# A hybrid recurrent trunk on one core: norm roots in two pieces among z's slabs, FFN tiles split in one pipeline, the result turned by halves

## The reference

```
def _gdn_mixer(x, conv0, S0, P, j):
    proj = x @ P['gdn_w_in'][j]                  # q | k | v | z | beta, decay
    qkv, conv_new = _causal_conv(proj[..., :GDN_CONV_DIM], conv0, P['gdn_conv_w'][j])
    qkv = silu(qkv)
    q = _l2norm(q heads) * GDN_DK ** -0.5
    k = _l2norm(k heads)
    ...
    o, S = _gated_delta_chunked(q, k, v, g, beta, S0)
    o = _rmsnorm(o, P['gdn_norm_w'][j]) * silu(gate)      # gate is z
    return o @ P['gdn_w_o'][j], conv_new, S

def _conv_ffn(x, conv0, P, i):
    h, conv_new = _causal_conv(x @ P['ffn_w_up'][i], conv0, P['ffn_conv_w'][i])
    return (silu(h[..., D_FF:]) * h[..., :D_FF]) @ P['ffn_w_down'][i], conv_new
```

## Time and profile before

| | |
|---|---|
| timed runs | 2292.86, 2284.80, 2296.56 us; median 2292.86 |
| the profiled execution | 2283.04 us; span from first to last instruction 2281.3 us |
| mean granted clock of TensorE | 0.939 |
| busy share of the span | PE 90%, PEld 83%, DVE 65%, ACT 43%, POOL 24% |
| DMA | 257.77 MB, mean 113 GB/s |
| GDN's input projection | ends near 788 us |
| the four FFNs start | near 387, 954, 1432 and 2040 us |
| the last residual tile | near 2270.6 us |

### The profile page before, as it was taken

One profiled execution on the slowest core, in us unless ns is written; L12 is line 12 of the kernel. 1 busy time (PEld: TensorE's weight loads), 2 busy tenths in 40 slices (PEclk: granted clock), 3 DMA queues, 4 the chain that ended last, 5 costly groups with the idle time before them and its releaser, 6 DMA issues.

```text
span 2281.3 us, 54685 instructions
## 1 busy us (share of the span) xinstructions
PE 2055.3 (90%) x23459; PEld 1891.9 (83%) x23459; DVE 1483.9 (65%) x2211; ACT 974.1 (43%) x1657; POOL 550.4 (24%) x934
## 2 busy tenths in 40 slices
PE   4999988999899787899989797999979899789997
PEld 3898867999778675799979776899958788679997
DVE  4785454896467556499645674898267655549963
ACT  3641134554456303455535434555345411345543
POOL 8000000453023211046201450365000200005520
PEclk9999998999989879899999888999979899989999
DMA  3430122555333323255535253354434101225542
GB/s 97 145 117 23 30 67 76 165 164 163 115 100 123 114 61 90 76 165 166 164 121 159 92 164 120 111 167 158 131 94 152 65 22 32 69 74 167 167 154 79
DMA packets 272112, 257.77 MB, mean 113 GB/s; under 512 B 30708, under 2 KB 267222, under 8 KB 271870
## 3 DMA queue, kind: packets, MB, share of 16 engines
q1 hardware_dynamic: 221472, 219.49, 30.0%
q10 hardware_dynamic: 45870, 20.44, 3.4%
q0 software_dynamic: 4528, 14.33, 2.3%
HBM read 235.69 MB, written 18.54 MB: 111 GB/s over the span
## 4 chain that ended last, share of the span: by engine, by line
PE 53%; DVE 6%; ACT 3%; issue 2%; ACTq 1%; POOL 0%; DMA 0%; DVEq 0%; POOLq 0%
PE wide L537 7%; PE wide L538 7%; PE wide L539 7%; PE bank L537 7%; PE bank L539 6%; PE bank L538 6%; DVE arena L2519 3%; PE wide L548 1%; PE wide L737 1%; DVE arena L2516 1%; PE wide L722 1%; PE wide L734 1%; ACT arena L1744 1%; PE bank L488 1%; PE wide L488 1%
## 5 line engine op out<-in xcount | busy, mean ns | idle before, releaser
L2519 DVE TENSOR_TENSOR w_lo<-ring,w_hi 128x2048 fp32r<-128x2048 f32 (+1 forms) x208 | 477.9, 2299 | 301.0 <-ACT w_hi L1744 298.1
L537 PE MATMUL wide<-arena_rounded,w_hi 128*128 128x288 f32 x1632 | 497.5, 305 | 51.6 <-DVE arena_rounded L2519 35.1
L537 PE MATMUL bank<-arena_rounded,w_hi 128*128 128x288 f32 x1632 | 491.2, 301 | 11.4 <-issue 11.4
L538 PE MATMUL wide<-arena_rounded,w_hi 128*128 128x288 f32 x1632 | 490.4, 300 | 0.0
L539 PE MATMUL wide<-arena_rounded,w_lo 128*128 128x288 f32 x1632 | 488.8, 300 | 0.0
L538 PE MATMUL bank<-arena_rounded,w_hi 128*128 128x288 f32 x1632 | 486.3, 298 | 0.0
L539 PE MATMUL bank<-arena_rounded,w_lo 128*128 128x288 f32 x1632 | 485.1, 297 | 0.0
L1744 ACT ACTIVATE w_hi<-ring 128x2048 fp32r<-128x2048 f32 (+1 forms) x208 | 391.6, 1884 | 141.1 <-PE bank L539 71.4
L537 PEld LDWEIGHTS wide<-arena_rounded,w_hi 128*128 128x128 f32 x1632 | 315.1, 193 | 64.9 <-issue 41.6
L537 PEld LDWEIGHTS bank<-arena_rounded,w_hi 128*128 128x128 f32 x1632 | 311.1, 191 | 12.8 <-issue 11.9
L2516 DVE SCALAR_TENSOR_TENSOR arena<-arena,pv 128x304 f32<-128x304 f32 (+2 forms) x512 | 303.3, 602 | 25.1 <-ACT arena L1744 9.6
(11 more groups left out here) (486 smaller groups left out, 2698.8 us busy)
## 6 DMA issues: line engine op xcount, KB each, us to landing
ring<-in_ffn_w_up SPq DMA_DIRECT2D x88, 1024.0 KB, 5.1
ring<-in_ffn_w_down SPq DMA_DIRECT2D x32, 896.0 KB, 4.7
ring<-in_rwkv_w_rkv SPq DMA_DIRECT2D x24, 1024.0 KB, 5.3
ring<-in_ffn_w_down SPq DMA_DIRECT2D x16, 1024.0 KB, 5.1
ring<-in_gdn_w_in SPq DMA_DIRECT2D x16, 1024.0 KB, 5.7
ring<-in_hgrn_w_in SPq DMA_DIRECT2D x16, 1024.0 KB, 5.4
ring<-in_rwkv_w_o SPq DMA_DIRECT2D x8, 1024.0 KB, 5.1
sraw<-in_state_rwkv_wkv POOLq DMA_DIRECT2D x32, 128.0 KB, 3.1
```

Source lines behind the costliest of these rows:

```text
L537: nc.tensor.matmul(out, wh, xh, start=first, stop=False)
L538: nc.tensor.matmul(out, wh, xl, start=False, stop=False)
L2519: return V.tensor_tensor(out, a, b, op)
```

## The change

Three edits. In GDN, ScalarE's roots move from behind tile 21 to behind the last silu of v, and are made in two pieces, `SQ` and `H` apart: both Ln behind the table load, then the evacuations of tiles 26 and 27 and slab 15's high half, then both Exp, and only then the staging of the conv state. z is evacuated as it is, and one silu over all of `S[8]` follows its last tile. On VectorE `norm_q_k` is gone; slab 15's low half stands ahead of the operands, and q and k are multiplied by their roots there. In the FFN the multiplications and subtractions of the eight tiles are interleaved, a subtraction two tiles behind. At the end the halves are the outer loop: the first halves of all three blocks need only four residual tiles; six banks are used, the third block is staged in `sout`, and the wait for the first two transfers is gone.

```diff
@@ TensorE, the end
-            pe.wait_ge(sem("x_ready"), after(pe, "x_ready", 2 * DEPTH * KC))
-            for blk, n in enumerate((P, P, NS)):
-                for q in range(2):
-                    b = 2 * (blk % 2) + q
+            for q in range(2):
+                pe.wait_ge(sem("x_ready"), (2 * DEPTH - 1) * KC + 4 * (q + 1))
+                for blk, n in enumerate((P, P, NS)):
+                    b = 3 * q + blk
                     pe.wait_ge(*freed(b))
@@ ScalarE, gdn
                     if n == 21:
                         raw_stats(H)
-                        log_and_exp()
-                        both = flat("H", 2)
-                        fn(both, both, ACT.Ln, bias=eps[:, 0:1]).then_inc(signal("scalar_chain"), 1)
-                        act.wait_ge(sem("scalar_chain"), told["scalar_chain"])
-                        fn(both, both, ACT.Exp, scale=-0.5).then_inc(signal("rk_ready"), 1)
-                        act.wait_ge(sem("rk_ready"), told["rk_ready"])
-                evac(S[8][:, 0, :], ACT.Silu)
                 qkv(GT - 2)
-                evac(S[8][:, 1, :], ACT.Silu)
+                evac(S[8][:, 0, :])
+                evac(S[8][:, 1, :])
                 split_hi(n0 + 14)
                 qkv(GT - 1)
+                log_and_exp()
+                for x in (SQ, H):
+                    fn(x, x, ACT.Ln, bias=eps[:, 0:1]).then_inc(signal("scalar_chain"), 1)
                 act.wait_ge(sem("saved"), after(act, "saved", 4))
-                evac(S[8][:, 2, :], ACT.Silu)
-                evac(S[8][:, 3, :], ACT.Silu)
+                evac(S[8][:, 2, :])
+                evac(S[8][:, 3, :])
                 split_hi(n0 + 15)
+                act.wait_ge(sem("scalar_chain"), told["scalar_chain"])
+                for x in (SQ, H):
+                    fn(x, x, ACT.Exp, scale=-0.5).then_inc(signal("rk_ready"), 1)
                 conv_state_out(OUT["prompt_gdn_conv"][0], OUT["sample_gdn_conv"][0], 72, 3)
                 for c in range(4, KC):
-                    evac(S[8][:, c, :], ACT.Silu)
+                    evac(S[8][:, c, :])
+                fn(S[8], S[8], ACT.Silu).then_inc(signal("z_gate"), 1)
+                act.wait_ge(sem("z_gate"), told["z_gate"])
                 log_and_exp()
@@ ScalarE, the end
-                if blk == 2:
-                    act.wait_ge(sem("y_out"), 32)
...
+            for q in range(2):
+                for blk, n in enumerate((P, P, NS)):
                     act.wait_ge(filled["scalar"], take())
-                    fn(tm[0:n, g, q * 512:(q + 1) * 512], psb()[0:n, :], ACT.Copy).then_inc(drained["scalar"], 1)
+                    fn(stages[blk][0:n, q * 512:(q + 1) * 512], psb()[0:n, :], ACT.Copy).then_inc(drained["scalar"], 1)
                     act.wait_ge(drained["scalar"], n_taken["n"])
...
+                    if q:
+                        act.dma_start(rows_out[blk], stages[blk][0:n, :]).then_inc(sem("y_out"), 16)
@@ VectorE, ffn
-                pre_norm("ffn_pre", i, "h_to_split")
-                for c in range(KC):
-                    dve.wait_ge(sem("x_hi"), after(dve, "x_hi"))
-                    tt(act3r("H")[:, c, :], H[:, c, :], act3r("A4")[:, c, :], ALU.subtract).then_inc(signal("x_split"), 1)
+                dve.wait_ge(sem("rstd_ready"), after(dve, "rstd_ready"))
+                for step in range(KC + 2):
+                    if step < KC:
+                        stt(H[:, step, :], X[:, step, :], pcol("ffn_pre", i, step), rstd[:, :]).then_inc(signal("h_to_split"), 1)
+                    if step >= 2:
+                        dve.wait_ge(sem("x_hi"), after(dve, "x_hi"))
+                        tt(act3r("H")[:, step - 2, :], H[:, step - 2, :], act3r("A4")[:, step - 2, :],
+                           ALU.subtract).then_inc(signal("x_split"), 1)
@@ VectorE, gdn
-                    if n == 22:
-                        norm_q_k()
...
-                tt(QG, Q, EG).then_inc(signal("vector_chain"), 1)
+                split_lo(n0 + 15)
+                dve.wait_ge(sem("rk_ready"), after(dve, "rk_ready"))
+                stt(Q, Q, float(P) ** -0.5, SQ).then_inc(signal("vector_chain"), 1)
+                dve.wait_ge(sem("vector_chain"), told["vector_chain"])
+                tt(QG, Q, EG)
+                dve.wait_ge(sem("rk_ready"), after(dve, "rk_ready"))
+                tt(K, K, H).then_inc(signal("vector_chain"), 1)
                 dve.wait_ge(sem("vector_chain"), told["vector_chain"])
                 stt(EG, K, -1.0, EG).then_inc(signal("operands_ready"), 1)
                 dve.wait_ge(sem("operands_ready"), told["operands_ready"])
-                split_lo(n0 + 15)
@@ VectorE, gated
-                    dve.wait_ge(drained["scalar"], mark["gin", 31] + 1)
+                    dve.wait_ge(sem("z_gate"), 1)
```

More of the change, by code:

```diff
@@ L2477, in _ @@
             ffn(3)
-            y = tm[:, :, :]
             hear_conv_out()
-            for blk, n in enumerate((P, P, NS)):
-                g = blk % 2
-                if blk == 2:
-                    act.wait_ge(sem("y_out"), 32)
-                for q in range(2):
+            hear_state_out()
+            stages = (tm[:, 0, :], tm[:, 1, :], sout)
+            rows_out = (OUT["y_prompt"][0][0:P], OUT["y_prompt"][0][P:2 * P], OUT["y_sample"].rearrange("b t f -> (b t) f"))
+            for q in range(2):
+                for blk, n in enumerate((P, P, NS)):
                     act.wait_ge(filled["scalar"], take())
-                    fn(tm[0:n, g, q * 512:(q + 1) * 512], psb()[0:n, :], ACT.Copy).then_inc(drained["scalar"], 1)
+                    fn(stages[blk][0:n, q * 512:(q + 1) * 512], psb()[0:n, :], ACT.Copy).then_inc(drained["scalar"], 1)
                     act.wait_ge(drained["scalar"], n_taken["n"])
-                dst = OUT["y_prompt"][0, blk * P:blk * P + n] if blk < 2 else OUT["y_sample"].rearrange("b t f -> (b t) f")
-                act.dma_start(dst, tm[0:n, g, :]).then_inc(sem("y_out"), 16)
+                    if q:
+                        act.dma_start(rows_out[blk], stages[blk][0:n, :]).then_inc(sem("y_out"), 16)
             act.wait_ge(sem("y_out"), 48)
@@ L3032, in exponents @@
                 dve.wait_ge(sem("exponents_ready"), told["exponents_ready"])
-            def norm_q_k():
-                dve.wait_ge(sem("rk_ready"), after(dve, "rk_ready"))
-                stt(S[1], S[1], float(P) ** -0.5, SQ)
-                tt(S[4], S[4], H).then_inc(signal("vector_chain"), 1)
-                dve.wait_ge(sem("vector_chain"), told["vector_chain"])
             def masks(hb, q):
```

## The result

The changed kernel takes 2267.11 us in the median of 8 runs, the kernel before 2290.03 in 8 runs of the same comparison: a ratio of 0.9914, 95% interval 0.9890 to 0.9939, or 14 to 25 us less. (The ratios here are those on record for each comparison; they aren't the quotients of the two medians, which lie 22.9 us apart here, and microseconds given with an interval go by the ratio.) 2279 (2270 to 2290) was forecast, so the kernel is faster, as the likeliest class said, but by more than the 11.9 us of the sum, and the time lies 2.9 us under the range.

A forecast was written before the change was run, and what follows sets the result against it. TensorE, busy 90% of the span, was taken as the bound, so time is won only where it stands still or runs slow. Gains of 6.4 + 1.2 + 4.3 = 11.9 us gave 2279 us from 2290.9, range 2270 to 2290.

The forecast's parts named there:

- the likeliest class: Whole kernel: faster by over 0.5%, chance 0.51, against 0.46 for within 0.5% and 0.03 for slower.
- the 11.9 us of the sum: Whole kernel: gains of 6.4 us in GDN, 1.2 in four FFNs and 4.3 at the end; bounds 8.7 to 13.3.
- The clock's 1.9 us: GDN, slabs 14 and 15: time lost to TensorE's 1.2 GHz clock after the long stop, taken between 1.4 and 2.4 us.
- 766.4: GDN: time in us at which slab 14 was to start on TensorE, after ScalarE's staging starts at 765.6.
- the lower bound of nothing: FFN starts: gain of 0 instead of 1.2 us, if the clock rises at a fixed time anyway.
- The bound of 2.8: The end: gain of only 2.8 us if the last transfer starts only when the block before it has landed.
- the one of 4.8: The end: upper bound, a gain of 4.8 us if TensorE's clock stays up through the turn.
- (1): GDN: VectorE becomes the bound, two of four products at 5.89 us; whole gain 7.3 us, 2283.6 us; chance 0.06.
- (2): GDN: GpSimd busy throughout, split and four products take 27.5 us; kernel 1.1 us slower, 2292.0 us; chance 0.03.
- The clock (4): GDN: clock stays at 1.2 GHz through both slabs after the long stop; whole gain 3.1 us, 2287.8; chance 0.02.
- the two rows 4: Profile rows cited for TensorE's clock after stops: 0.53 over 3.22 us in GDN, 0.50 over 5.40 us at an FFN's start.
- Rival (3): GDN: table switch holds ScalarE longer, staging 1.3 us later; whole gain 10.6 us, 2280.3 us; chance 0.07.

The follow-up runs named there:

- the version with the roots on both sides: Changed kernel with query roots ahead of the conv state's staging, key roots behind it, query product before slab 15's split: 2265.34 us (0.9925), again 2270.59 us (0.9938).
- the trace with five products: Changed kernel with one VectorE product in GDN (the gated query) made twice in a row: 2273.72 us in 1 run.
- the second and the third comparison: Changed kernel rerun unaltered against the kernel before: 2271.05 us for 2283.34 (0.9934), then 2271.97 us for 2284.04 (0.9947).
- GDN alone: Kernel before with only the change's GDN edit (roots, z, slab 15's split): 2280.30 us for 2283.34, ratio 0.9985.
- the rest alone: Kernel before with the FFN and end edits, without the GDN edit: 2278.06 us for 2284.04, ratio 0.9974.
- the version with the roots behind the staging: Changed kernel with ScalarE's staging of the conv state ahead of both Ln and both Exp: 2272.24 us for 2285.60, ratio 0.9947.

## Why the prediction was right, and where it was not

**GDN, 6.4 forecast, 6.7 measured.** Matmul starts of the two traces are 3.1 us apart at the start of the stage. With that, slab 13's split was put to end at 752.0 and ended at 752.0; ScalarE's staging was put at 765.6 + 3.1 = 768.7 and came at 768.45; the stop was put at about 9 us and is 8.60; the inversion was put at 781.75 + 3.1 = 784.85 and came at 784.60. The clock's 1.9 us is what the window shows, but that it fits is luck: it was picked between 1.4 and 2.4 with no row to decide, and the premise that the clock is low after such stops holds for some of them only. Behind the kernel before's own 2.22 us stop the clock stayed at 1.00, and behind the 2.84 us stop of the version with the roots on both sides 3.05 us were lost. A small slip is hidden as well: 766.4 leaves 0.28 us for the three transposes behind the staging, which take 0.51 (768.97 to 769.48), and the staging came 0.25 us earlier than put. The products ended 1.0 us before slab 15 (783.95), where 1.4 was forecast, and 1.7 before the inversion.

**FFN, 1.2 forecast, 1.2 measured at the first matmul.** Later in the stage it is less steady. From the start of that wait to the 41st matmul of the second FFN the five traces without the edit have 12.69 to 12.73 us; of the nine with it four have 12.51 to 12.55, so 0.2 of the 0.3 stay there, two 12.28 and 12.36, and three 11.33 to 11.45. Nothing of it can be seen at the end of a longer stretch: from the inversion's first matmul to the 15486th, in which the second and the third FFN start, the two traces with the FFN edit and GDN's roots in their old place take 810.6 and 810.7 us, the four without the edit 810.6 to 810.8. So the size is right at the starts, but whether it reaches the end isn't shown, and the lower bound of nothing stands.

**The end, 4.3 forecast, 3.9 measured.** The last issue comes 3.97 us after the last residual tile (2271.03 less 2266.60 + 0.46), where it came 8.35 us after it (2278.94 less 2270.59): 4.4 less, as worked out. The span goes on for 2.85 us after that issue where it went on for 2.37, so 0.5 was lost behind it, put down here to transfers issued close together, which no run tests by itself, and for which 0.1 had been set aside. That term was mis-sized, by 0.4 us. The bound of 2.8 (the last transfer behind the one before it) was not met; the one of 4.8 (the clock up through the turn) nearly was, once: in the trace with five products the twelve transposes behind the last tile take 1.53 us for 2.82, and the end is 4.4 us shorter than before.

**The rivals.** VectorE's products ran at 2.5 to 2.56 us each, so neither (1) nor (2) came about; GpSimd waits for slab 15 for 26.57 us there, as it did before. The clock (4) was back after 3.76 us; the two rows 4, which the prediction set against it, stop where the low stretch does and hardly show its return. Rival (3) fell as well: after the table load at 756.22, 1.28 us, the Ln begins at 757.51, 0.01 us behind its end, and ScalarE was busy up to 756.22. The Trainium skill (ScalarE: Activation LUTs, "What ACT_TABLE_LOAD costs") gives 1283 ns for the load, which agrees, and about 1380 ns of drain for every switch, which isn't in any trace here. The same section prices an ACTIVATE higher when its bias is read from a per-partition operand: the Ln with eps takes 2.21 to 2.22 us and the Exp, which has none, 2.12 to 2.13 in the version with the roots apart.

**What missed is the time, through the scatter that the range left out.** The step was "I predict 2279 us, which lies between the two and puts the kernel before at 2290.9", with a range drawn from "the fastest timed run less the largest gain". The base was right for the comparison that it was made for: the kernel before came out at 2290.03. What the forecast missed there is the difference, 14 to 25 us by the ratio for 11.9, and "some gain above 13.3 that I have not seen" had a chance of only 0.03. The later comparisons speak for chance in the two medians of 8 as most of it. In them the kernel before has medians of 2283 to 2286 and the changed one 2271 to 2272, so in the first comparison the one came out 4 to 7 us high and the other 4 to 5 us low. Four runs between 2283 and 2297 had stood for the kernel; in the 92 runs of the three later comparisons it takes 2268 to 2298. A median of 8 moves by several us with that, and the range held none of it. The gain of 11.9 lies inside the intervals of the second and the third comparison (15.1 and 12.1) and below that of the first.

**What stays open.** Three comparisons together say 12 to 19 us, the stages 11.8. The parts add up to less, not more: GDN alone and the rest alone give 3.4 + 5.9 = 9.3 us. In the comparison that had the three parts and the whole side by side they give 3.4 - 1.1 + 3.0 = 5.3 us, where the whole has 15.1. With about 5 us on either side of each part that can be scatter, but that the parts win more together than alone isn't excluded. No trace shows a place outside the three stages that the change shortens on every execution. The stretch behind GDN isn't quite untouched, though. From the inversion to the 15486th matmul the six traces with the roots in their old place take 810.6 to 810.8 us, while the four with the change's GDN take 814.2, 814.8, 814.9 and 807.1: the same work, with other courses of the clock (in the 814.8 and 814.9 the granted clock is 0.92, in the 807.1 and in the kernel before's 810.7 it is 0.93). The version with the roots on both sides takes 816.1 us there in one of its traces and 808.7 in the other. Whether that averages out over many executions, and so whether the change is worth 12 or 15, these runs don't settle.

## What to carry to other kernels

Work out each stop from its own queue, instruction by instruction: here that gave 6.4, 1.2 and 4.3 us for 6.7, 1.2 and 3.9. A stop costs its length and the slow clock behind it, and the second part can be as large as the first (1.87 us of stop, 3.6 us of time) or nothing (the 2.22 us stop of the kernel before): look at the granted clock behind each. Judge a change of half a per cent by its stages in the trace, where GDN and the FFN starts repeat to 0.04 us, and look at what the stretches behind them make of it. Take the range of the time from as many executions of the kernel before as can be had, not from the spread of three.

## What the runs showed of the hardware

- The GDN stage with the same instructions repeats to within 0.04 us from one execution to the next (50.27 to 50.31, five traces with GDN as before; 43.56 to 43.58, four with the change's), while whole executions of one kernel differ by up to 29 us. Not every stage repeats so well: the end takes 13.5 us in eight traces with its edit and 13.0 in the ninth, and the stretch behind GDN 807.1 to 814.9 in four with the same GDN. The longer the clock was at 1.2 GHz in an execution, the longer it took (correlation -0.91 with the mean granted clock in 29 runs), and per length the most of it arises in the first 110 us, where 99.1 to 110.3 us were taken for the same 500 matmuls.
- The length of a stop doesn't tell what it costs in clock. Behind 8.60 us of standing still the clock was low for 3.76 us of work, behind 2.84 us for 6.1 (in both traces). Behind 2.22 us it stayed at 1.00 in the kernel before and was at 0.50 for 3.3 us of work in the version with the roots behind the staging; behind 1.87 us it was at 0.57 over 4.00 us.
